# One stage for the gated recurrence of prompt and samples, the experts' rows added by TensorE, and one group of modulation weights moved to an earlier stage

## The chip, the cores and the metric

The kernel runs on one NeuronCore of one Trainium2 chip. The metric is the device time of one execution in microseconds; the kernel before has a median of 1935.73 us over three runs. Five engines work side by side: PE (TensorE, matmuls; its weight loads are PEld), DVE (VectorE), ACT (ScalarE), POOL (GpSimd) and SP (SyncE, which here only issues transfers). Each works through its own queue in program order, and semaphores order them among each other. PE's clock is granted at one of two levels, 1.2 or 2.4 GHz; the profile shows it as 0.5 or 1.

## The reference, cut to what matters

A step of a two-layer decoder, all in float32: a prompt of 512 tokens and 8 samples of one token each, width 1024. Layer 0 mixes by gated linear attention, layer 1 by differential attention over a cache; each layer ends with a mixture of 16 experts, of which every token takes two.

```python
def gla_recurrent(q, k, v, g, s0):          # the 8 samples, one step
    s = jnp.exp(gt)[..., None] * s + kt[..., None] * vt[..., None, :]
    return s, jnp.einsum('bhk,bhkv->bhv', qt, s)
...
sh1, sc1, g1, sh2, sc2, g2 = jnp.split(c @ w_ada[l] + b_ada[l], 6, axis=-1)
x = layer_norm(DEEPNORM_ALPHA * x + g1[:, None, :] * mix, ln_mix_g[l], ln_mix_b[l])
xm = modulate(x, sh2, sc2)
ff = moe_ffn(xm, w_router, b_router, w_exp_gate[l], w_exp_up[l], w_exp_down[l])
x = layer_norm(DEEPNORM_ALPHA * x + g2[:, None, :] * ff, ln_ffn_g[l], ln_ffn_b[l])
```

The state of the samples is 8 batches x 4 heads, each 128 x 256.

## The kernel before

The program is a row of stages, each a block whose engines all meet at its end: modulation, projection, recurrence of the prompt, recurrence of the samples, output (`stage_mix_output`), routing, experts, combine, decoder (layer 1's attention), and again output, routing, experts, combine. Tokens stand in five tiles (`TILES`): four of 128 and one of 8.

**Recurrence, prompt** (L593 on). Four chunks. DVE makes decays and factors, ACT their exponents (L720 to L726), PE transposes (L758), scores (L764 to L771), the new state's products (L780) and outputs (L788, L789); DVE adds the state (L688) and ACT copies outputs (L736). SP first fills unused slots of `y_rows` (L805), waits for that transfer, and then loads the samples' states (L590), 4 MB.

**Recurrence, samples** (`stage_gla_sample`). For every batch PE spreads the values over 128 partitions (L881, two banks of 512 columns), DVE decays the state (L859) and adds key times value (L863), four heads each; then PE multiplies the new state by the query (L890), and SP stores it (L832). The output weights load here (L905). At the end DVE copies the output rows (L869).

**Output.** PE projects a tile at a time (L1070); DVE gates, normalises and modulates (L1111 to L1130, L1011 to L1016); PE turns the modulated rows (L1060). SP writes the rows out, one transfer of 512 KB per tile, which the experts gather later (L941); these buffers alternate, so that tile n's row waits for the transfer of tile n - 2. `m.v` and `m.r`, in the upper part of `arena_w`, are read for the last time when the fifth tile has been turned.

**Routing.** PE makes the logits (L1261, L1266); DVE works 11 us on the choice of experts, then PE counts (L1272). Meanwhile SP loads five 2 MB pieces of the first experts' weights (L1170).

**Combine** (`stage_combine`). POOL gathers the two experts' rows of a tile (L1694), two tiles ahead of use. ACT multiplies the first by its weight (L1730), DVE adds the second times its weight (L1708), gates (L1111), adds the residual (L1119), takes the moments (L1123, L1125); ACT normalises (L1153), DVE multiplies by the gain (L1138, one tile late) and POOL adds the bias (L1144). In layer 0 the stage also makes two groups of modulation vectors (class `Ada`, `ada_groups=(8, 10)`): for each a bias and four 2 MB pieces of `w_ada` are loaded (L190, L192) and PE multiplies them (L203, L207). Group 10's four pieces are not loaded before group 8's products are done.

## Time and profile before

| | us |
|---|---|
| median of three runs (lowest, highest) | 1935.73 (1934.38, 1936.28) |
| the profiled execution's own time | 1931.71 |
| its span, first to last instruction | 1929.8 |
| recurrence, both stages | 284.6 to 370.0 |
| output and routing of layer 0 | 370.0 to 496.7 |
| experts of layer 0 | 496.7 to 812.7 |
| combine of layer 0 | 812.7 to 884.1 |
| decoder | 884.1 to about 1415 |
| output, routing and experts of layer 1 | about 1415 to 1871.1 |
| combine of layer 1 | 1871.1 to 1929.8 |

In a timeline row stand the start, the duration, the engine, the line, the operation, what it writes and reads, how many such instructions the row joins, and in brackets how long the engine sat idle before it and who ended that. A float32 matmul shows as two records, so that x32 are 16 matmuls.

### The profile page before, as it was taken

To read this page: it belongs to the slowest core of one execution; us is meant where nothing else is said; L and a number is where in the kernel's file an instruction comes from. 1 tells how busy PE (TensorE), PEld (TensorE's weight loads), DVE (VectorE), ACT (ScalarE), POOL (GpSimd) and SP (SyncE) were. 2 spreads that over 40 slices of the span, in tenths; PEclk is the share of its full clock that TensorE was granted. 3 is DMA by queue.
4 is the path that set the end of the run, shared out by engine and by line. 5 is a ranking of instruction groups with operands and counts; after the bars stand their busy time and mean duration, and the time that the engine had idled before them with its cause. 6 is when DMAs were issued, how large, how long until landed. Compare 5 with 4: busy or idle time off the path is not lost. (4 is left out here: it accounts for less than half of the span.)

```text
span 1929.8 us, 22099 instructions
## 1 busy us (share of the span) xinstructions
PE 1521.2 (79%) x7374; PEld 709.2 (37%) x7375; DVE 733.9 (38%) x1284; ACT 418.1 (22%) x908; POOL 349.3 (18%) x270
## 2 busy tenths in 40 slices
PE   5899986695689999646999887777596599989950
PEld 2333335142333333203466563444343233333320
DVE  1001127675300000075846577995275300000018
ACT  1001014221121222222120002334431021212222
POOL 0000000000100000033735566650000000000004
PEclk8999998597799999967999997888798699999985
DMA  8572604604599999699789999985503499999962
GB/s 314 225 275 111 263 36 152 233 23 185 224 425 422 392 382 427 275 370 344 276 306 402 408 383 412 351 316 182 186 17 129 188 417 384 418 420 400 430 242 89
DMA packets 123149, 551.66 MB, mean 286 GB/s; under 512 B 16469, under 2 KB 46022, under 8 KB 101419
## 3 DMA queue, kind: packets, MB, share of 16 engines
q1 hardware_dynamic: 94530, 492.46, 64.4%
q10 hardware_dynamic: 19584, 37.28, 5.1%
q0 software_dynamic: 8944, 20.76, 3.0%
q8 instruction: 51, 0.84, 0.2%
q14 instruction: 40, 0.33, 0.0%
HBM read 521.82 MB, written 40.03 MB: 291 GB/s over the span
## 5 line engine op out<-in xcount | busy, mean ns | idle before, releaser
L1576 PE MATMUL ps<-arena_w,arena_r 128*64 128x512 f32 x1600 | 361.7, 608 | 28.8 <-issue 23.9
L1576 PEld LDWEIGHTS ps<-arena_w,arena_r 128*64 128x64 f32 x1600 | 121.1, 140 | 262.6 <-issue 256.5
L1558 PE MATMUL ps<-arena_w,arena_r 128*64 128x512 f32 x800 | 181.5, 601 | 19.4 <-ACT arena_r L1606 19.4
L1653 DVE TENSOR_TENSOR arena_r<-arena_r,ps 128x512 f32<-128x512 f32 x38 | 26.1, 687 | 419.1 <-ACT arena_r L1623 419.1
L1959 POOL TENSOR_TENSOR arena_w<-arena_w,arena_r 128x1024 f32<-128x1024 f32 x48 | 115.5, 2409 | 104.0 <-DMA arena_w<-in_cache_k_dram 103.7
L1959 POOL TENSOR_TENSOR arena_r<-arena_r 128x1024 f32<-128x1024 f32 x48 | 115.9, 2418 | 54.7 <-DMA arena_r<-in_cache_k_dram 54.6
L2012 PE MATMUL ps<-arena_w,xt 128*128 128x256 f32 x512 | 123.4, 403 | 1.4 <-ACT xt L2185 1.4
L450 PE MATMUL ps<-arena_w,xt 128*128 128x512 f32 x256 | 113.8, 600 | 1.0 <-DVE arena_w L531 0.6
L1070 PE MATMUL ps<-arena_w,xt 128*128 128x512 f32 x256 | 111.4, 593 | 0.0
L2012 PEld LDWEIGHTS ps<-arena_w,xt 128*128 128x128 f32 x512 | 102.5, 203 | 17.9 <-ACT xt L2185 1.5
L1507 POOL COPY small<-idx 128x1 int32 (+1 forms) x38 | 7.0, 184 | 516.9 <-PE ps L1524 456.0
L1558 PEld LDWEIGHTS ps<-arena_w,arena_r 128*64 128x64 f32 x800 | 54.8, 138 | 119.9 <-issue 98.1
L1646 DVE COPY arena_r<-ps 128x512 f32<-128x512 f32 x38 | 26.3, 691 | 186.9 <-PE ps L1558 186.9
L1622 ACT ACTIVATE arena_r<-ps 64x512 f32<-64x512 f32 x38 | 22.4, 589 | 338.2 <-PE ps L1576 338.2
L2347 DVE TENSOR_REDUCE arena_r<-arena_w 128x16 f32<-128x1024 f32 x64 | 76.6, 1212 | 23.5 <-POOL arena_w L1959 23.4
L2347 DVE TENSOR_REDUCE arena_r<-arena_r 128x16 f32<-128x1024 f32 x64 | 76.6, 1210 | 17.3 <-POOL arena_r L1959 17.2
L2024 PE MATMUL ps<-arena_m,arena_r 128*16 128x512 f32 x512 | 67.8, 652 | 7.2 <-DMA arena_m<-in_cache_v_dram 7.2
L450 PEld LDWEIGHTS ps<-arena_w,xt 128*128 128x128 f32 x256 | 48.0, 191 | 66.3 <-issue 65.6
L1070 PEld LDWEIGHTS ps<-arena_w,xt 128*128 128x128 f32 x256 | 48.0, 190 | 59.1 <-issue 59.1
L415 PE MATMUL ps<-xt,arena_w 128*128 128x512 f32 x128 | 59.1, 616 | 4.0 <-PEq L249 3.7
L1234 POOL MEMSET arena_r<- 128x2048 f32 x2 | 3.6, 1806 | 308.1 <-POOLq L927 308.1
L2004 PE MATMUL ps<-xt,arena_w 128*128 128x512 f32 x128 | 56.9, 601 | 0.0
(384 smaller groups left out, 1969.5 us busy)
## 6 DMA issues: line engine op xcount, KB each, us to landing
arena_w<-in_w_exp_gate_dram SPq DMA_DIRECT2D x38, 2048.0 KB, 13.6
arena_w<-in_w_exp_up_dram SPq DMA_DIRECT2D x38, 2048.0 KB, 19.1
arena_w<-in_w_exp_down_dram SPq DMA_DIRECT2D x38, 2048.0 KB, 17.5
arena_m<-in_cache_v_dram SPq DMA_DIRECT2D x128, 512.0 KB, 7.0
arena_w<-in_cache_k_dram SPq DMA_DIRECT2D x64, 512.0 KB, 9.0
arena_r<-in_cache_k_dram SPq DMA_DIRECT2D x64, 512.0 KB, 8.4
arena_w<-in_w_ada_dram SPq DMA_DIRECT2D x12, 2048.0 KB, 17.6
arena_m<-in_w_ada_dram SPq DMA_DIRECT2D x12, 2048.0 KB, 9.2
```

Source lines behind the costliest of these rows:

```text
L415: last = nc.tensor.matmul(m.ps[n % 2][:, :], w, m.xt[:, k, 0:SEQ], start=(k == 0), stop=(k == KT - 1))
L450: last = nc.tensor.matmul(m.ps[4 + n % 4][:, :], m.xt[:, k, i * P:(i + 1) * P], m.wr[c % 2][:, k, :], start=(k == 0), stop=(k == KT - 1))
L1070: last = nc.tensor.matmul(m.ps[(4 if n % 2 else 6) + c][0:r, :], m.xt[:, k, i * P:i * P + r], w.of(k, c), start=(k == 0), stop=(k == KT - 1))
L1558: last = nc.tensor.matmul(psy[c][at:at + 64, :], ht[u][:, k, 64 * (1 - a):64 * (2 - a)], wd[u][:, k, c * 512:(c + 1) * 512], start=(k == 0 ...
L1576: last = nc.tensor.matmul(ps[at:at + 64, :], xgt[u][:, k, 64 * a:64 * (a + 1)], w[u][:, k, :], start=(k == 0), stop=(k == KT - 1), tile_po ...
L1646: V.tensor_copy(ys[u][:, 0:512], psy[0][:, :]).then_inc(y_v, 1)
L1653: V.tensor_tensor(hs[u], es[u], psu[:, :], ALU.mult).then_inc(h_ok, 1)
L1959: G.tensor_tensor(kp[n % RING], kp[n % RING], qb[b % 2], ALU.mult).then_inc(pp_ok, 1)
L2004: last = nc.tensor.matmul(bank[:, :], w[:, k, part * P:(part + 1) * P], m.xt[:, k, 0:SEQ], start=(k == 0), stop=(k == KT - 1))
L2012: last = nc.tensor.matmul(bank[:, i * CW:(i + 1) * CW], m.xt[:, k, t], w[:, k, :], start=(k == 0), stop=(k == KT - 1))
L2024: last = nc.tensor.matmul(PSO[n][32 * g:32 * g + C, :], PR[b % 2][:, GRP * q + g, :], vp[GRP * (v % 2) + g][:, n * 512:(n + 1) * 512], sta ...
L2347: V.tensor_reduce(out=S[b % 2][:, j, :], in_=kp[n % RING].rearrange("p (c d) -> p c d", d=DHB), axis=AX.X, op=ALU.add).then_inc(ks_ok, 1)
```

## The change

It has four parts, and one that goes with them. (1) Prompt and sample recurrence are one stage, `stage_gla`. The states load first and the fill of `y_rows` after them, from another source, awaited only at the end. A sample's output is computed from the old state with decayed queries, plus the product of query and key times the value; a sample's state takes one product of PE (K = 8 rows) and one operation of DVE that decays and adds. The products use seven banks of PSUM, and two alternating banks for transposed keys become one. Four copies on ACT and four selections on POOL prepare the masked keys. The output weights load in four parts. (2) The combine of both layers scales and adds the two rows on PE, by diagonal matrices that ACT makes from the weights; the normalisation is two operations of DVE. POOL only gathers, and gathers again once PE has read the rows. (3) Group 10 of `Ada` loads in layer 0's output stage, between the store of the first and the second tile, and is multiplied in the routing, after the logits and before the counts. (4) The first experts' up and down weights wait for these products, since they use the same buffers. In the routing POOL's clearing of a buffer moves to the end.

```diff
+            def sample(u):
+                b, h = u // HA, u % HA
+                if h == 0:
+                    v.wait_ge(st_in[b // 2], 16)
+                    wait(v, so_mm, 1 - b)
+                v.wait_ge(kv_mm, u + 1)
+                V.scalar_tensor_tensor(out=st[:, u, :], in0=st[:, u, :], scalar=eg[:, h, b:b + 1], in1=kv_ps[u % 7],
+                                       op0=ALU.mult, op1=ALU.add).then_inc(st_ok, 1)
...
             state(2)
+            for u in range(3):
+                sample(u)
             state(3)
+            for u in range(3, NS * HA):
+                sample(u)
+            sample_rows()
...
             key_rows(1)
+            s.wait_ge(kr_mm, 1)
+            for h in range(HA):
+                nc.scalar.copy(masked[h], so_ps[32 * h:32 * h + NS, 0:P].unsqueeze(1).to_broadcast([NS, NS, P])).then_inc(kr_ok, 1)
             exponents(2)
...
                 pe.wait_ge(fac_ok, i + 1)
-                wait(pe, kl_ok, i - 1)
+                wait(pe, kl_ok, i)
...
+            def sample(u):
+                b, h = u // HA, u % HA
+                wait(pe, st_ok, u - 6)
+                nc.tensor.matmul(kv_ps[u % 7], masked[h][:, b, :], m.v[32 * h:32 * h + NS, NTT - 1, h * DVA:(h + 1) * DVA],
+                                 start=True, stop=True, tile_position=(32 * h, 0)).then_inc(kv_mm, 1)
...
             outputs(1)
+            sample_outputs()
             factors(2)
             factors(3)
             outputs(2)
+            pe.wait_ge(ks_ok, HA)
+            pe.wait_ge(kl_ok, NTL)
+            pe.wait_ge(at_ok, NTL)
+            for u in range(3):
+                sample(u)
             outputs(3)
+            pe.wait_ge(s_ok, NTL)
+            pe.wait_ge(o_ev, NTL)
+            for u in range(3, NS * HA):
+                sample(u)
@@ stage_mix_output
                 sp.dma_start(m.xmD[i * P:i * P + r, :], xm[n % 2][0:r, :]).then_inc(rows_out[n % 2], 16)
+                if n == 0 and ada is not None:
+                    sp.wait_ge(tr, NTT)
+                    for step in range(Ada.STEPS):
+                        ada.load(sp, step)
@@ stage_route
-            load_expert(sp, m, weights, 0, 0)
-            load_expert(sp, m, weights[0:2], 1, 1)
+            load_expert(sp, m, weights[0:1], 0, 0)
+            load_expert(sp, m, weights[0:1], 1, 1)
+            if ada is not None:
+                sp.wait_ge(ada.used, Ada.STEPS)
+            load_expert(sp, m, weights[1:3], 0, 0)
+            load_expert(sp, m, weights[1:2], 1, 1)
...
             last.then_inc(mm, 1)
+            if ada is not None:
+                for step in range(Ada.STEPS):
+                    ada.product(pe, step)
             pe.wait_ge(sel_ok, 1)
@@ stage_combine
+            for i, r in TILES:
+                pe.wait_ge(dg_ok, i + 1)
+                pe.wait_ge(y_in[i % 2], 32 * (i // 2 + 1))
+                wait(pe, f_ok, i - 1)
+                for n in range(2):
+                    for c in range(2):
+                        last = nc.tensor.matmul(y_ps[i % 2][n][0:r, :], dg[c][i][0:r, 0:r], y[i % 2][c][0:r, n * 512:(n + 1) * 512],
+                                                start=(c == 0), stop=(c == 1))
+                last.then_inc(y_mm, 1)
+                if i:
+                    for step in range((i - 1) * steps // (NTT - 1), i * steps // (NTT - 1)):
+                        ada.product(pe, step)
...
                 if i >= 2:
-                    g.wait_ge(f_ok, i - 1)
+                    g.wait_ge(y_mm, i - 1)
...
-                v.wait_ge(y1_ok, i + 1)
-                y1, y2 = y[i % 2]
-                nc.vector.scalar_tensor_tensor(out=y1[0:r, :], in0=y2[0:r, :], scalar=m.wts[0:r, 1, i:i + 1],
-                                               in1=y1[0:r, :], op0=ALU.mult, op1=ALU.add)
-                v.drain()
-                ln.mixed(v, i, r, [y1[:, 0:512], y1[:, 512:1024]]).then_inc(f_ok, 1)
-                ln.stats(v, i, r)
-                if i:
-                    ln.shift(v, *TILES[i - 1])
-            ln.shift(v, *TILES[-1])
+                v.wait_ge(y_mm, i + 1)
+                ln.mixed(v, i, r, y_ps[i % 2]).then_inc(f_ok, 1)
+                ln.normalised(v, i, r)
@@ build
-        stage_combine(nc, ctx, m, 0, a, ada_groups=(8, 10), vectors=(6, 7, 12, 13), dec=dec)
+        stage_combine(nc, ctx, m, 0, a, ada_groups=(8,), vectors=(6, 7, 12, 13), dec=dec)
```

Three places where instructions stand otherwise. The first is DVE at the end of the recurrence. Before, from the last scores to the output rows (L688 adds the prompt's state, L859 and L863 the samples'; the pair of rows comes eight times):

```order
L679 TENSOR_TENSOR arena_r<-ps,arena_r 128x512 x2
L688 SCALAR_TENSOR_TENSOR arena_w<-arena_w,small,ps 128x256 x8
L626 UNCONDITIONAL_BRANCH
L850 UNCONDITIONAL_BRANCH
L852 MEMSET arena_r 128x256
L854 COPY arena_r<-arena_w 128x4x8
L859 TENSOR_SCALAR arena_m<-arena_m,arena_r 128x256 x4
L863 SCALAR_TENSOR_TENSOR arena_m<-ps,arena_w,arena_m 128x256 x4
```

and with the change (L736 adds the prompt's state, L675 is the one operation per sample and head, L685 the output rows):

```order
L727 TENSOR_TENSOR arena_r<-ps,arena_r 128x512 x2
L736 SCALAR_TENSOR_TENSOR arena_w<-arena_w,small,ps 128x256 x4
L675 SCALAR_TENSOR_TENSOR arena_m<-arena_m,arena_w,ps 128x256 x3
L736 SCALAR_TENSOR_TENSOR arena_w<-arena_w,small,ps 128x256 x4
L675 SCALAR_TENSOR_TENSOR arena_m<-arena_m,arena_w,ps 128x256 x29
L680 COPY arena_w<-ps 128x1
L685 SCALAR_TENSOR_TENSOR arena_w<-arena_w,ps 8x256 x4
```

The block's end between the two parts is gone, and 64 operations on the states are 32, three of them ahead of the prompt's last state. The second place is SP's queue in layer 0's output stage, before (-) and after (+):

```order
-L941 DMA xm_rows<-arena_r 8x1024
-L941 DMA xm_rows<-arena_r 128x1024 x4
+L962 DMA arena_r<-in_w_router_dram 128x8x16
+L962 DMA arena_r<-in_b_router_dram 128x16
+L965 DMA xm_rows<-arena_r 8x1024
+L190 DMA arena_r<-in_b_ada_dram 1x2048
+L192 DMA arena_w<-in_w_ada_dram 128x2x2048 x4
+L965 DMA xm_rows<-arena_r 128x1024 x4
```

The four 2 MB loads stand ahead of four of the five row stores. The third is PE in layer 0's combine, before

```order
L203 MATMUL ps<-arena_r,ones 32x512 x4
L207 MATMUL ps<-arena_w,small 32x512 x32
L203 MATMUL ps<-arena_r,ones 32x512 x4
L207 MATMUL ps<-arena_w,small 32x512 x32
L1684 MATMUL ps<-ident,arena_r 128x9 x32
```

and after (L1739 are the diagonal products, four a tile):

```order
L1739 MATMUL ps<-arena_r,xt 128x512 x8
L203 MATMUL ps<-arena_r,ones 32x512 x4
L207 MATMUL ps<-arena_w,small 32x512 x8
L1739 MATMUL ps<-arena_r,xt 128x512 x4
L207 MATMUL ps<-arena_w,small 32x512 x8
L1739 MATMUL ps<-arena_r,xt 128x512 x4
L207 MATMUL ps<-arena_w,small 32x512 x8
L1739 MATMUL ps<-arena_r,xt 8x512 x4
L207 MATMUL ps<-arena_w,small 32x512 x8
L1750 MATMUL ps<-ident,arena_r 128x9 x32
```

One group's products are gone, and the others stand between the tiles' sums, each behind the next tile's.

## Rows read from the trace of the kernel before

**Rows 1.** Layer 0's combine: us, busy PE, PEld, DVE, ACT, POOL; clock, DMA share, GB/s.

```profile
812.70:884.10 71.40, 29.79 (x176) 7.79 (x176) 42.52 (x59) 15.64 (x18) 26.70 (x15) 0.62 0.93 358
```

**Rows 2.** Timeline of DVE, 332 to 368 us: start us, us, line, op, tiles.

```profile
332.08 1.66 DVE L688 SCALAR_TENSOR_TENSOR arena_w<-arena_w,small,ps 128x256 f32<-128x256 f32 x4 [3.53 <-PE ps L780]
...
343.75 1.66 DVE L863 SCALAR_TENSOR_TENSOR arena_m<-ps,arena_w,arena_m 128x256 f32<-128x256 f32 x4 [2.12 <-PE ps L881]
...
366.37 1.72 DVE L869 COPY arena_w<-ps 8x256 f32<-8x256 f32 x4 [1.16 <-PE ps L890]
```

**Rows 3.** Waits of DVE, 285 to 385 us: total us, times, longest.

```profile
DVE arena_m L863 <- PE ps L881: 2.6, 3, 2.1
```

**Rows 4.** Timeline of SP's queue in the same stages.

```profile
296.30 5.95 SPq L590 DMA_DIRECT2D arena_m<-in_state_gla_dram  x4
...
370.04 0.30 SPq L336 DMA_DIRECT2D arena_m<-mod_rows  x1
```

**Rows 5.** Timeline of PE in the same stages.

```profile
316.17 0.66 PE L758 MATMUL ps<-ident,arena_w 128*128 128x128 f32 x4 [2.86 <-DVE xt L674]
...
345.46 1.04 PE L890 MATMUL ps<-arena_m,arena_r 128*8 128x256 f32 x8
...
346.43 2.08 PE L881 MATMUL ps<-arena_w,arena_r 8*128 8x512 f32 x4
```

**Rows 6.** Timeline of ACT in the same stages.

```profile
304.83 0.63 ACT L720 ACTIVATE arena_w<-arena_r 128x512 f32<-128x512 f32 x1 [2.08 <-DVE arena_r L659]
...
335.54 1.07 ACT L736 COPY arena_w<-ps 128x512 f32<-128x512 f32 x2 [4.11 <-PE ps L789]
```

**Rows 7.** Timeline of DVE in layer 0's output stage.

```profile
440.58 1.23 DVE L1011 TENSOR_TENSOR arena_r<-x_res,arena_m 128x1024 f32<-128x1024 f32 x1 [1.31 <-ACT x_res L1153]
...
448.89 1.29 DVE L1111 TENSOR_TENSOR arena_r<-ps,arena_m 128x512 f32<-128x512 f32 x2 [3.35 <-PE ps L1070]
```

**Rows 8.** Timeline of PE in layer 0's output stage and routing.

```profile
418.04 1.04 PE L1060 MATMUL ps<-ident,arena_r 8*128 8x8 f32 x8
...
434.95 13.90 PE L1070 MATMUL ps<-arena_w,xt 128*128 128x512 f32 x32
...
481.12 0.71 PE L1272 MATMUL ps<-arena_r,ones 128*128 128x80 f32 x2 [10.93 <-DVE arena_r L1365]
...
505.13 1.12 PE L1576 MATMUL ps<-arena_w,arena_r 128*64 128x512 f32 x2 [1.16 <-ACT arena_r L1600]
```

**Rows 9.** Timeline of PE in layer 0's combine, to the decoder's start.

```profile
824.69 1.93 PE L203 MATMUL ps<-arena_r,ones 1*32 1x512 f32 x8 [16.61 <-DMA arena_w<-in_w_ada_dram]
...
826.55 3.64 PE L207 MATMUL ps<-arena_w,small 128*32 128x512 f32 x16
...
831.84 1.92 PE L207 MATMUL ps<-arena_w,small 128*32 128x512 f32 x16 [1.65 <-DMA arena_w<-in_w_ada_dram]
...
884.18 1.02 PE L2104 MATMUL ps<-ident,x_res 8*128 8x8 f32 x8 [4.95 <-PEq L57]
```

**Rows 10.** Timeline of ACT in layer 0's combine.

```profile
824.08 1.15 ACT L1730 ACTIVATE arena_r<-arena_r,wts 128x1024 f32<-128x1024 f32 x1 [14.79 <-DMA arena_r<-y_rows,dest]
...
831.65 1.15 ACT L1730 ACTIVATE arena_r<-arena_r,wts 128x1024 f32<-128x1024 f32 x1 [6.42 <-DMA arena_r<-y_rows,dest]
```

**Rows 11.** Timeline of SP's queue in layer 0's combine.

```profile
848.78 0.25 SPq L190 DMA_DIRECT2D arena_r<-in_b_ada_dram  x1
```

**Rows 12.** Timeline of DVE in layer 1's combine.

```profile
1902.92 1.28 DVE L1708 SCALAR_TENSOR_TENSOR arena_r<-arena_r,wts 128x1024 f32<-128x1024 f32 x1
...
1904.28 3.27 DVE L1111 TENSOR_TENSOR arena_r<-arena_r,arena_m 128x512 f32<-128x512 f32 x2
...
1912.32 1.27 DVE L1708 SCALAR_TENSOR_TENSOR arena_r<-arena_r,wts 8x1024 f32<-8x1024 f32 x1
```

**Rows 13.** Timeline of ACT in layer 1's combine.

```profile
1878.62 1.15 ACT L1730 ACTIVATE arena_r<-arena_r,wts 128x1024 f32<-128x1024 f32 x1 [10.90 <-DMA arena_r<-y_rows,dest]
```

**Rows 14.** Timeline of SP's queue at the end.

```profile
1927.65 0.34 SPq L1757 DMA_DIRECT2D out_y_sample_dram<-x_res  x1
```

More of the change, by code:

```diff
@@ L698, in _ @@
             differences(1)
+            decayed_queries()
             products(0)
@@ L812, in _ @@
             sp.wait_ge(s_out, 16)
[L815 to L828 removed]
+            sp.wait_ge(o_mm, NTL)
@@ L1288, in _ @@
             nc.scalar.activation(E, L, ACT.Exp).then_inc(ex_ok, 1)
+            if ada is not None:
+                ada.evacuate(s, nc.scalar.copy, 0)
+                ada.store(s, 0)
+                ada.finish(s)
         @block.vector
@@ L1676, in _ @@
         def _(pe):
-            for step in range(len(ada_groups) * Ada.STEPS):
-                ada.product(pe, step)
+            steps = len(ada_groups) * Ada.STEPS
+            for i, r in TILES:
[10 more added lines that the diff above has]
+                        ada.product(pe, step)
             for n, row in enumerate(rows):
```

229 lines of the change are left out of this document (115 added, 114 removed).

## The prediction, written before the changed kernel ran

> **What bounds the kernel now.** I read the stretches by stage first, then each engine's timeline in the stages that the change touches, and last the waits. No engine bounds the whole: every stage ends at its own wait, and what is saved in one moves the next forward whole, since all engines meet at a block's end. The samples' recurrence fills the time from the prompt's last state, 333.74, to 370.04: DVE starts its first four L863 at 343.75 and the output copies L869 at 366.37, eight batches of four L859 and four L863, 2.8 us each [rows 2], with 2.6 us of waiting for PE in all [rows 3]; the next stage's first transfer is issued at 370.04 [rows 4]. Layer 0's combine takes 71.4 us with the transfer engines 93% busy [rows 1], with 16 MB of modulation weights in it. Layer 1's combine has no such weights: from 1878.62, when the first gathered rows are there [rows 13], to the last store's issue at 1927.65 [rows 14], it is a chain of DVE, 9.40 us from one tile's L1708 to the next's [rows 12]. In layer 0's output stage PE sets the pace (32 records of L1070 in 13.90 us, then DVE waits 3.35 us for PE) [rows 7, 8], and from there on the transfers are nearly idle until the routing.
>
> **Term 1, the recurrence: 12.9 us saved.** The new stage goes on from where the prompt's part goes now, but the prompt's part itself gets later. ACT makes four copies of 8 x 1024 out of PSUM. Two copies of 512 columns take 1.07 us [rows 6], so each costs about that, 4.3 us together; ACT idles 2.08 us before the exponents L720 that follow [rows 6], so these and the output copies behind them come 2.3 us later, and PE's second outputs wait for that copy. PE then makes the samples' outputs: 8 batches of L890's form, 1.04 us each at the lower clock [rows 5], 8.3 us; the clock here is the higher one for most of the time, and I take 4.4 us. PE idles 2.86 us before the next transposes at 316.17 [rows 5], which come 3.7 us later by this (2.3 + 4.4 - 2.86 = 3.8). DVE's fourth factors come 1.9 us later through ACT, and PE's last scores are held by both; I carry 2.1 us. The one bank for transposed keys costs nothing: the copy that it waits for is 0.58 us long and stands behind 3 us of factors on DVE. The last prompt state ends at 332.08 + 1.66 = 333.74, ACT's last copies at 336.6 [rows 2, 6]; both 2.1 us later, and three samples' products (1.3 us) go ahead: PE begins the other 29 at 340.0. DVE's operation reads one SBUF and one PSUM tile as L863 does, 1.66 / 4 = 0.41 us, with 0.40 from start to start. So 29 x 0.40 = 11.6 and 0.6 for the first hand-over give 352.2; the sum and four short operations (L869's four take 1.72) end at 354.6, and the last state's store, at 355. Now the block goes on 370.04 - 368.09 = 1.95 us after DVE's last copy [rows 2, 4]; so 357.1, 12.9 us earlier. Bounds: PE at the lower clock for the outputs, 4 us more delay, 9; no delay of the prompt's part, 15.5. The states load at once, not 11.7 us later [rows 4]; they were not waited for in either case. The output weights come in four parts, the last one at about 349, and are read some 10 us into the next stage: nothing.
>
> **Term 2, layer 0's output stage: 0.** SP waits until the fifth tile is turned, 419 [rows 8], and then issues four 2 MB loads; the store of the second tile stands behind them in the same queue, with 2.3 us of issuing and 8.4 MB of data ahead. At the 0.41 MB/us of the busy stretches that is 20 us, so the store lands at about 441. DVE rewrites that buffer at 440.58 and has 3.35 us to spare before the last tile [rows 7]. Bound: 29 us for the loads, since in layer 0's combine, beside gathers, the second piece comes 7.15 us after the first [rows 9]; the store lands at 451; 10.4 - 3.35 = 7 us lost.
>
> **Term 3, the routing: 0.** PE is done with the logits at 470.2 and waits 10.93 us for DVE [rows 8]. The group costs a bias of 1.93 us and four steps of 3.64 (lower clock) or 1.92 (higher) [rows 9]: 9.6 to 16.5 us. In the combine the clock rises after the first step, so I take 1.9 + 1.9 + 3 x 1.92 = 9.6: hidden, with 1.3 us to spare. Without it, 16.5 - 10.93 = 5.6 us come on the path, since the counts stand behind the products in PE's queue and DVE waits for them. The first up and down weights are issued at 480, 15 us later, and three pieces take 15.7 us: 496, before the experts' first product at 505.13 [rows 8]. ACT's copy and stores end there too.
>
> **Term 4, layer 0's combine: 7 us saved.** Group 10's loads are gone, that begin at 848.78 [rows 11], when group 8's products are done, and hold the transfers to the end. What sets the end then? The first rows still land at 824.08 and the second at 831.65 [rows 10], as the transfers are as loaded as before: 8.4 MB of group 8, then at once 4.2 MB for the decoder and 4.2 MB of gathers, all done at 854 at 0.42 MB/us. PE adds a tile in four matmuls, 8 records; of L1070's form 32 take 13.90 us [rows 8], so 3.5 us at 2.4 GHz and 7.0 at 1.2 GHz. PE has been idle and starts low: 6.1 us for the first, and DVE begins at 830.3, not 825.3. Then the gathers hold it: a gather is issued when PE has read the tile before the last, and lands some 10 us after its issue under load. So the third tile is there at 844 and summed at 848.5, the fourth (behind a step of the group, 1.9 to 3.6 us) at 855.5, the fifth landed at 857.8 and summed at 863. DVE takes 7 us for it, ACT copies and stores the group's rows, and the stage ends at 873. PE idles 4.95 us before the decoder's first matmul at 884.18 [rows 9], some 4 us of it after the stage's end; so 877, 7 us earlier. Bounds: 13 (all sums at the higher clock, gathers in time: 824.1 + 3.5 + 5 x 6.94 + 4 = 866.3, and 4 for the group's rows and the stage change: 871) and 2 (the lower clock throughout, PE alone 56 us).
>
> **Term 5, layer 1's combine: 8.3 us saved.** A tile of DVE: 9.40 [rows 12] less L1708 (1.36 with its drain), less 1.98 (L1111's two take 3.27 beside POOL [rows 12] and 1.29 out of PSUM [rows 7]), less 0.08 and the 0.29 us wait for ACT, plus one 1024-wide operation of 1.25: 6.94 us. The start: rows at 1878.6, PE cold 6.1 us, 1884.8; five tiles end at 1919.5, and the last store goes out there, not at 1927.65 [rows 14]: 8.2, and 8.3 with the shorter tail. Bounds: 5 (each sum at 7.0 us, gathers chained behind it) and 11 (first sum 3.5 us). ACT's ten diagonal copies lie before 1878.6, with 10.9 us of idling there [rows 13]; were they on the path they would cost about 3 us.
>
> L1111 takes 3.27 us only in tiles in which POOL's L1144 runs. The Trainium skill (SBUF — State Buffer, "SBUF: two separate sides") says that DVE and GpSimd share one port pair as an exclusive lock, and that a gather issued from GpSimd needs it for its descriptors. The trace agrees for L1144; by that page the gathers remain a contender, which would leave some of the 1.98 us in.
>
> Speaking against the change, the lower clock: PE's first group step takes 3.64 us and the next 1.92 [rows 9]. The Trainium skill (TensorE: Matmul & The Clock Gate, "What's actually happening") says that the throttled 1.2 GHz is the default and activity releases it. If that kept PE low in a stage where it works under half of the time, terms 4 and 5 would be 2 and 5: the first rival.
>
> **Sum.** 12.9 + 0 + 0 + 7 + 8.3 = 28.2. The profiled execution took 1931.71 us, so 1903.5; the median of the runs is 4.0 above it, and I forecast 1906 for a median.
>
> **The rivals.**
> (a) PE stays at 1.2 GHz in the combines and gathers chain behind it: 12.9 + 2 + 5 = 20, so 1916. For it: granted clock 0.62 in layer 0's combine [rows 1]; against it: 831.84's step at 1.92 after an idle gap [rows 9]. 0.20.
> (b) The row stores land late behind the loads, 7 us, perhaps with the routing's 5.6: 28.2 less 7 to 12.6, 1913 to 1919. The Trainium skill (DMA: Bandwidth & Descriptors, "Queues, rings and completion order") has descriptors of one ring consumed in order; no row shows a small store behind large loads. 0.12.
> (c) More comes: the terms' upper bounds, 15.5 + 12 + 10 = 37.5, so 1898. 0.16.
> (d) Slower: the samples' loop does not run ahead. Seven banks part PE from DVE; if each of the 29 still costs a matmul (0.6 to 1.1) and an operation (0.41) in turn, 1.6 us each are 46 us for 11.6: 34.8 lost against 28.2, so 6.6 us above the median, 1942. It decides from 28.2 / 29 + 0.40 = 1.37 us a sample on. Against it: DVE waited for L881 only 2.6 us in eight batches, with two banks of lead [rows 3], and a pair of L881's takes PE 1.04 us for two heads [rows 5]. 0.03.
>
> **Numbers.** The forecast (24 to 33 us, 1901 to 1911) has 0.48, with (a) 0.20, (c) 0.16, (b) 0.12, (d) 0.03, and 0.01 for a change that comes to nothing. The range of 1894 to 1918 leaves out half of (b)'s tail, (d) and the far end of (c). A measurement of this kernel tells 0.2%, 3.9 us, from nothing: faster 0.96, same 0.01, slower 0.03.
>
> **What the changed profile would show.** Right: the output stage's first transfer near 357; the sample operations 0.40 us apart without waits; PE's counts in the routing still at 481 less 13; tiles of 7 us in the combines, and L1111 never above 1.4; the decoder 20 us earlier, the last store's issue 28 us earlier. Wrong if: sums of 7 us on every tile; DVE waiting before the fourth tile of the output stage; PE still at L192's products when DVE has chosen; or the samples' operations further than 0.5 us apart.

## The result, and the profile after

The changed kernel took 1907.19 us (median of 3 runs, 1902.56 to 1916.82), the kernel before 1935.73: a ratio of 0.9866, with a 95% interval of 0.9818 to 0.9913, so 28.5 us less. The forecast was 1906, in a range of 1894 to 1918. The profiled execution of the changed kernel took 1907.19 us, with a span of 1905.3. One run further down (the one with the output weights last) took 2032.78 us at a granted clock of 0.79, where its kernel otherwise shows 0.89 to 0.90, and is left out of that kernel's median.

Both profiles cut at the same places, each stage from its first transfer or first instruction to that of the next (us; the last one to the last store's issue). Each column is one execution; the experiments show how far a stage with the same code moves between executions, 2 to 8 us in the longest ones:

| stage | before | after | difference | forecast |
|---|---|---|---|---|
| recurrence | 85.5 | 75.8 | -9.7 | -12.9 |
| layer 0's output stage | 93.1 | 94.8 | +1.7 | 0 |
| layer 0's routing and experts | 349.5 | 352.2 | +2.7 | 0 |
| layer 0's combine | 71.5 | 60.0 | -11.5 | -7 |
| decoder, layer 1's output stage | 599.7 | 598.3 | -1.4 | 0 |
| layer 1's routing and experts | 387.9 | 390.4 | +2.5 | 0 |
| layer 1's combine | 55.8 | 47.2 | -8.6 | -8.3 |

**Recurrence.** The timelines of DVE and of SP's queue after (start us, us, line, op, tiles, idle time before), to be held against [rows 2, 4]:

```profile
339.98 11.45 DVE L675 SCALAR_TENSOR_TENSOR arena_m<-arena_m,arena_w,ps 128x256 f32<-128x256 f32 x29 [3.72 <-PE ps L853]
351.35 0.15 DVE L680 COPY arena_w<-ps 128x1 f32<-128x1 f32 x1
351.58 1.94 DVE L685 SCALAR_TENSOR_TENSOR arena_w<-arena_w,ps 8x256 f32<-8x256 f32 x4
```

```profile
340.49 3.50 SPq L903 DMA_DIRECT2D out_s_sample_dram<-arena_m  x3
344.10 0.49 SPq L929 DMA_DIRECT2D arena_w<-in_w_o_a_dram  x1
345.19 6.64 SPq L903 DMA_DIRECT2D out_s_sample_dram<-arena_m  x5
360.22 0.30 SPq L336 DMA_DIRECT2D arena_m<-mod_rows  x1
```

DVE takes 11.45 us for 29 heads, 0.395 each, in one row without a gap: PE runs ahead as forecast. But DVE is done at 353.5, and the next stage begins only 6.7 us later, where it was 1.95 before. The waits of SP's queue say for what (total us, times, longest):

```profile
SPq L917 <- DMA out_s_sample_dram<-arena_m: 6.4, 1, 6.4
```

The queue's owner waits 6.4 us for the last state's store to land; that store stands behind 1 MB of output weights and four other stores of 0.5 MB in one queue. Before the change the same wait was

```profile
SPq L826 <- DMA out_s_sample_dram<-arena_m: 2.6, 1, 2.6
```

**Layer 0's output stage.** DVE after, against [rows 7]:

```profile
425.21 1.29 DVE L1139 TENSOR_TENSOR arena_r<-ps,arena_m 128x512 f32<-128x512 f32 x2 [5.73 <-PE ps L1098]
...
435.78 1.23 DVE L1039 TENSOR_TENSOR arena_r<-x_res,arena_m 128x1024 f32<-128x1024 f32 x1 [5.56 <-DMA xm_rows<-arena_r]
440.66 1.28 DVE L1139 TENSOR_TENSOR arena_r<-ps,arena_m 128x512 f32<-128x512 f32 x2
```

The row store behind the group's four loads is awaited 5.56 us, in place of 1.31 us for ACT. The 3.35 us for PE that stood before the last tile are used up, so that 4.25 - 3.35 = 0.9 us lie on the path. The rest of the stage's 1.7 us has nothing to do with the loads, which are issued at 409. It lies in PE's products of the modulation vectors at the stage's start, before the change and after it:

```profile
380.87 4.69 PE L154 MATMUL ps<-arena_w,xt 128*32 128x512 f32 x32
```

```profile
371.04 5.47 PE L154 MATMUL ps<-arena_w,xt 128*32 128x512 f32 x32
```

The same 32 records take 4.11 to 5.56 us in the profiles of the other kernels, with and without the loads.

**Routing.** PE after, against [rows 8]:

```profile
461.99 1.93 PE L203 MATMUL ps<-arena_r,ones 1*32 1x512 f32 x8
463.85 8.58 PE L207 MATMUL ps<-arena_w,small 128*32 128x512 f32 x64
472.77 0.50 PE L1321 MATMUL ps<-arena_r,ones 128*128 128x80 f32 x2 [0.34 <-DVE arena_r L1418]
```

The group's products lie under DVE's choice of experts: PE still waits 0.3 us for DVE behind them. The granted clock was 0.50 for the bias and the first of them (461.9 to 466.0) and 0.93 for the rest.

**Layer 0's combine.** PE after, against [rows 9], and one row of windows (columns as in [rows 1]):

```profile
818.76 5.24 PE L1739 MATMUL ps<-arena_r,xt 128*128 128x512 f32 x8 [16.16 <-DMA arena_r<-y_rows,dest]
826.42 3.67 PE L1739 MATMUL ps<-arena_r,xt 128*128 128x512 f32 x8 [2.42 <-DMA arena_r<-y_rows,dest]
...
836.94 6.38 PE L1739 MATMUL ps<-arena_r,xt 128*128 128x512 f32 x8 [4.00 <-issue]
...
852.79 3.78 PE L1739 MATMUL ps<-arena_r,xt 8*8 8x512 f32 x8 [2.13 <-issue]
...
867.24 1.01 PE L2156 MATMUL ps<-ident,x_res 8*128 8x8 f32 x8 [3.93 <-PEq L57]
```

```profile
807.20:867.20 60.00, 35.80 (x144) 13.24 (x144) 33.79 (x54) 6.04 (x17) 11.95 (x11) 0.76 0.77 285
```

The transfers are busy 77% of the stage instead of 93%: they no longer fill it to its end. They still hold it in one place. The third tile's gather is issued when PE has read the first tile, and DVE waits for its sum:

```profile
843.36 1.29 DVE L1139 TENSOR_TENSOR arena_r<-ps,arena_m 128x512 f32<-128x512 f32 x2 [5.25 <-PE ps L1739]
```

Three of the sums take 3.7 to 3.8 us, the other two 5.2 and 6.4.

**Layer 1's combine.** DVE's first and last tile, and the last store, against [rows 12, 14]:

```profile
1868.15 1.29 DVE L1139 TENSOR_TENSOR arena_r<-ps,arena_m 128x512 f32<-128x512 f32 x2 [12.79 <-PE ps L1739]
...
1875.16 1.28 DVE L1139 TENSOR_TENSOR arena_r<-ps,arena_m 128x512 f32<-128x512 f32 x2
...
1896.09 1.27 DVE L1139 TENSOR_TENSOR arena_r<-ps,arena_m 8x512 f32<-8x512 f32 x2
```

```profile
1903.10 0.34 SPq L1809 DMA_DIRECT2D out_y_sample_dram<-x_res  x1
```

One tile to the next takes 7.0 us instead of 9.4, and DVE waits for nothing after its first.

### The profile page after: what moved, and what is told of

Same layout as the page of the kernel before. It is cut to its first block and busy times, and to the rows that moved or that the text cites. A ratio compares the mean times of both kernels' runs of the same rounds, so it can differ in the third digit from the quotient of the medians.

```text
span 1905.3 us, 22323 instructions
## 1 busy us (share of the span) xinstructions
PE 1556.4 (82%) x7502; PEld 729.9 (38%) x7503; DVE 704.6 (37%) x1243; ACT 404.9 (21%) x914; POOL 320.0 (17%) x262
## 5 line engine op out<-in xcount | busy, mean ns | idle before, releaser
L1629 PE MATMUL ps<-arena_w,arena_r 128*64 128x512 f32 x1600 | 365.8, 614 | 28.6 <-issue 23.7
L1611 PE MATMUL ps<-arena_w,arena_r 128*64 128x512 f32 x800 | 183.4, 606 | 19.3 <-ACT arena_r L1659 19.3
L2011 POOL TENSOR_TENSOR arena_r<-arena_r 128x1024 f32<-128x1024 f32 x48 | 115.4, 2410 | 56.5 <-DMA arena_r<-in_cache_k_dram 56.2
L1739 PE MATMUL ps<-arena_r,xt 128*128 128x512 f32 (+1 forms) x80 | 42.7, 687 | 41.4 <-DMA arena_r<-y_rows,dest 30.5
```

The costliest lines, as they stand in the source:

```text
L1611: last = nc.tensor.matmul(psy[c][at:at + 64, :], ht[u][:, k, 64 * (1 - a):64 * (2 - a)], wd[u][:, k, c * 512:(c + 1) * 512], start=(k == 0 ...
L1629: last = nc.tensor.matmul(ps[at:at + 64, :], xgt[u][:, k, 64 * a:64 * (a + 1)], w[u][:, k, :], start=(k == 0), stop=(k == KT - 1), tile_po ...
L1739: last = nc.tensor.matmul(y_ps[i % 2][n][0:r, :], dg[c][i][0:r, 0:r], y[i % 2][c][0:r, n * 512:(n + 1) * 512], start=(c == 0), stop=(c == 1))
L2011: G.tensor_tensor(kp[n % RING], kp[n % RING], qb[b % 2], ALU.mult).then_inc(pp_ok, 1)
```

## The experiments

Two theories stood at the start. The first is the prediction's: each term is a chain in its own stage, and layer 0's combine was held by the transfers of group 10. The rival: PE's sums and DVE's shorter row of work are what shortened that combine, and the group's place matters little. A second pair was about the 3 us missing in the recurrence: bytes ahead of the last store, or stores that are slow whatever stands ahead.

The kernels of one list shared a chip, and the kernel before ran beside each list: the first four; then the loads in pairs, the eight products, one bank and four pairs; then the last two. On the second chip the changed kernel itself was not run, so there a median is compared through its ratio to the kernel before (0.985 to 0.9866 for the changed kernel).

**The changed kernel again** (no edit).

> The changed kernel as it is, timed again in more rounds, because its three runs lay 14 us apart (1902.56 to 1916.82) where those of the kernel before lay 2 us apart. If the terms of the sum hold, 24.6 us earlier in the profile, the median is again 1904 to 1910. If the spread is its own (the experts' stage of layer 0 took 2.7 us more in the profile of after than before, at a clock of 0.96 against 0.98), single runs again lie 5 us or more above the fastest, and the difference shows in the long TensorE stages and not in the stages that were edited; if it was chance of one chip, the runs lie within 4 us.

Measured: 1906.15 us (5 runs, 1903.3 to 1910.08), ratio 0.985 (0.9826 to 0.9875). The kernel before, run 23 times beside the first four kernels, spread from 1927.1 to 1942.5, so three runs within 2 us say little, and the scatter is no property of the change. Where it comes from, the stage cuts show: over the profiles, in all of which their code is untouched, the decoder with layer 1's output stage lasts 597.1 to 604.9 us, layer 1's routing and experts 387.8 to 390.4. The +2.7 of layer 0's routing and experts is of this kind too: those stages take 352.1 us in the next kernel, in which they are exactly those of before. The recurrence varies too: 75.4 to 75.8 us in three of the profiles with its code unchanged, 77.1 in one, and 78.8 to 79.0 in three, this one among them. PE's timeline in this one:

```profile
304.79 1.99 PE L838 MATMUL ps<-arena_w,arena_r 128*128 128x256 f32 x8
310.09 3.78 PE L847 MATMUL ps<-arena_w,arena_r 128*128 128x256 f32 x8 [3.31 <-DVE arena_r L727]
313.66 3.17 PE L838 MATMUL ps<-arena_w,arena_r 128*128 128x256 f32 x8
```

In the first profile L847 takes 1.89 us there and the L838 behind it 1.97. After a wait of 3.31 us PE works at half its pace, 3.78 us for 1.89, and the products behind are slow too.

That wait has a cause in the rows, and it lies on POOL and DVE. POOL's selections of the masked keys, which are new with the change, run beside DVE's row of subtractions (L701 to L707). In the first profile they begin when only the last of these is still to come:

```profile
303.81 0.42 DVE L706 TENSOR_TENSOR arena_r<-arena_r 128x256 f32<-128x256 f32 x1
304.15 1.58 DVE L707 TENSOR_TENSOR arena_r<-arena_r 128x512 f32<-128x512 f32 x1
303.83 5.28 POOL L655 TENSOR_SCALAR_AFFINE_SELECT arena_w<-arena_w 8x1024 f32<-8x1024 f32 x4 [17.96 <-ACT arena_w L799]
```

and in this one three are still to come, and each of them takes 0.9 us longer; the operation that PE waits for, L727, stands behind them:

```profile
305.39 1.32 DVE L705 TENSOR_TENSOR arena_r<-arena_r 128x256 f32<-128x256 f32 x1
306.63 1.30 DVE L706 TENSOR_TENSOR arena_r<-arena_r 128x256 f32<-128x256 f32 x1
307.86 1.57 DVE L707 TENSOR_TENSOR arena_r<-arena_r 128x512 f32<-128x512 f32 x1
305.29 5.11 POOL L655 TENSOR_SCALAR_AFFINE_SELECT arena_w<-arena_w 8x1024 f32<-8x1024 f32 x4 [17.51 <-ACT arena_w L799]
```

All ten profiles of kernels with this stage divide the same way. In five, PE's second transposes (L816) take 1.11 or 1.12 us, POOL begins 1.03 us behind DVE's L701, and one operation of DVE is stretched. In the other five the transposes take 0.66 us, so that ACT and POOL come half a microsecond sooner, and three operations are stretched; these are the profiles with the stage at 77 us or more (75.8 in the one that has the output weights last). So it goes by the pace at which PE makes these transposes, and here the quicker transposes give the longer stage. That is read from the profiles; no run moved POOL's selections to prove it, and what decides PE's pace there stays open.

**The new combine alone**, on the kernel before: the combine and the normalisation's methods of the change, group 10 still in layer 0's combine.

```
 # the kernel before, with
 stage_combine, LayerNorm     # as changed
 stage_combine(..., 0, a, ada_groups=(8, 10), ...)   # as before
```

> The kernel before with the new combine alone; group 10 of the modulation weights is still loaded in layer 0's combine, and the recurrence is the old one. Theory 1 (as in the prediction, the transfers hold layer 0's combine while group 10 is in it): layer 1's combine gives 8.5 us, layer 0's at most 2, so 10 us less than before, 1925. Theory 2 (PE's sums and the shorter row of work on DVE are what shortened layer 0's combine, the group's place matters little): layer 0's combine about 61 us here too, 20 us less, 1916.

Measured: 1930.14 us (12 runs), beside 1934.02 for the kernel before; ratio 0.9976 (0.9959 to 0.9992). By stage, layer 0's combine takes 71.75 us (71.5 before), layer 1's 48.6 (55.8 before): theory 1. DVE in layer 0's combine:

```profile
856.53 1.29 DVE L1111 TENSOR_TENSOR arena_r<-ps,arena_m 128x512 f32<-128x512 f32 x2 [0.51 <-PE ps L1698]
870.82 1.28 DVE L1111 TENSOR_TENSOR arena_r<-ps,arena_m 8x512 f32<-8x512 f32 x2 [7.22 <-PE ps L1698]
882.10 0.22 DVE L1736 TENSOR_SCALAR small<-ps 128x64 f32<-128x64 f32 x1 [4.30 <-PE ps L1709]
```

PE's sum for the fifth tile stands in its queue behind two steps of group 10, which wait for their weights; DVE, faster per tile, now waits 7.22 us for it and 4.30 more at the end, for the products of the group's last weights. The transfers are busy 92% of the stage. All of the new combine's gain in layer 0 is lost in the waits for them.

**Group 10 back in layer 0's combine**, on the changed kernel.

```
-stage_mix_output(..., router, ada=ada)
-stage_route(..., router, ada=ada)
-stage_combine(..., ada_groups=(8,), ...)
+stage_mix_output(..., router)
+stage_route(..., router)
+stage_combine(..., ada_groups=(8, 10), ...)
```

> The changed kernel with group 10 back in layer 0's combine: no modulation load in the output stage, no products in the routing. Theory 1: layer 0's combine lasts 69 to 71 us again instead of 60, the output stage gets its 1.7 us back, so 8 us slower than the changed kernel, 1915. Theory 2: the combine stays near 61 us, and with the 1.7 us given back the time is 1905 to 1907, the same as the changed kernel. Under both the wait of DVE for the row store in the output stage (5.56 us) is gone.

Measured: 1922.71 us (12 runs), ratio to before 0.9943 (0.9925 to 0.9961). This is 16.6 us above the changed kernel on the same chip, twice what theory 1 gave. Its combine lasts 74.4 us instead of 60.0, and its output stage 92.9 instead of 94.8 (DVE waits 3.33 us for PE again, none for the row store): 12.5 us by stage. That figure is itself good to some 3 us, since the same combine lasted 71.75 us in the run before. The other 4 lie within the scatter of the later stages.

Along the steps before, new combine, new recurrence, moved group, the medians fall by 3.9, 7.4 and 16.6 us; by stage the same steps are about 7 (layer 1's combine), 10 and 12.5. The last step shifts 8 MB of loads into a stretch with idle transfers and saves nothing by itself in instructions, and it comes last: what it gives the old combine was not run. An estimate from the kernel before: its combine ends with an addition on POOL,

```profile
876.30 2.33 POOL L1144 TENSOR_TENSOR x_res<-x_res,arena_m 8x1024 f32<-8x1024 f32 x1 [1.15 <-DVE x_res L1138]
```

at 878.6, and with 2.1 us to the decoder, as after the change, it could not have ended before 880.7. So the move alone would be worth at most 3.5 us there and the new combine alone is worth nothing; the 11.5 us come only with both.

**Output weights behind the last store**, on the changed kernel.

```
-            w_out.load(sp, 0)
             for b in range(3, NS):
                 sample_store(b)
+            w_out.load(sp, 0)
```

> The changed kernel with one edit in the recurrence: the first part of the output weights (1 MB) is issued after the last state's store, not ahead of the last five. In the changed kernel the queue's owner waits 6.4 us for the last store to land (2.6 us before the change). Theory A (this tail is the 1 MB and the four stores ahead of the last one, by bytes in flight): 1 MB at 0.41 MB/us is 2.5 us, the wait falls to about 4 us, the next stage begins 2.5 us earlier, 1904.7, unless the weights, now 2.5 us later, are awaited there. Theory B (the stores' own landing is slow, whatever stands ahead of them): the wait stays at 6 us or more and the time is unchanged.

Measured: 1904.61 us (5 runs, 1901.49 to 1916.2), ratio 0.986 (0.9828 to 0.9892). In the profile the wait falls, as in theory A, and by more than its 2.5 us:

```profile
SPq L917 <- DMA out_s_sample_dram<-arena_m: 2.5, 1, 2.5
```

The recurrence lasts 72.6 us instead of 75.8, and the output stage 94.9, so its weights are not missed. From the last store's issue to the next stage it is 5.1 us instead of 8.4, where it was 4.4 before the change. The saving of 3.2 us is there in the stage and not to be told from nothing in the median (1.5 us less).

**Group's loads in two pairs**, on the changed kernel.

```
 if n == 0 and ada is not None:
     sp.wait_ge(tr, NTT)
-    for step in range(Ada.STEPS):
-        ada.load(sp, step)
+if n < 2 and ada is not None:
+    for step in range(2 * n, 2 * n + 2):
+        ada.load(sp, step)
```

> The changed kernel with the four 2 MB loads of group 10 in two pairs in the output stage: two behind the first tile's row store, two behind the second's. Theory A (rival b of the prediction: in one queue, the row store lands only behind the 8 MB ahead of it, and DVE's rewrite of the buffer waits, 5.56 us in the profile of the changed kernel of which 3.35 were idle before): DVE's wait for the row store goes, PE is again what DVE waits for, 3 us or so before the last tile, and the output stage is 93 us instead of 94.8, so 1 to 2 us less than the changed kernel. Theory B (what makes the stage longer is the load on the transfer engines as such, or the clock): no change, or the wait moves to the next tile's row store.

Measured: 1910.22 us (5 runs), ratio 0.9873 (0.9852 to 0.9893). In the stage, theory A: 92.6 us, and DVE waits as before the change:

```profile
429.41 1.23 DVE L1040 TENSOR_TENSOR arena_r<-x_res,arena_m 128x1024 f32<-128x1024 f32 x1 [1.31 <-ACT x_res L1194]
437.71 1.29 DVE L1140 TENSOR_TENSOR arena_r<-ps,arena_m 128x512 f32<-128x512 f32 x2 [3.34 <-PE ps L1099]
```

Of the 2.2 us by which the stage is shorter, 0.9 are the loads'. They are DVE's wait of 5.56 us less the idle time that was there anyway. The other 1.3 us are again PE's L154 at the stage's start, 4.14 us here and 5.47 in the first profile, ahead of the loads. The median did not follow: the five runs lie 8.8 us apart (1904.11 to 1912.89), and 1 us can't be read from them.

**Eight products before the first sum**, on the changed kernel (they go to an unused bank).

```
+            for n in range(8):
+                nc.tensor.matmul(m.ps[3][:, :], m.ident[:, :], m.lnr[:, 0, 0:512], start=True, stop=True)
             for i, r in TILES:
```

> The changed kernel with eight more 128x512 products of PE into an unused bank at the start of each combine, while PE waits 12 to 16 us for the first gathered rows (they add nothing to the result). Theory A (the first sums are slow because PE comes to them at the lower clock: the first takes 5.24 us, the second 3.67): the first sum takes 3.7 us in both combines, layer 1's combine is 1.5 to 2 us shorter, layer 0's not much, since the gathers hold its third tile; 1904. Theory B (the first sum is slow because the second gather of the tile lands late, not because of the clock): it stays at 5.2 us and the time at 1906. If the eight products end too early, the clock falls again before the rows land, and A shows less.

Measured: 1906.49 us (4 runs), ratio 0.9854 (0.9831 to 0.9877). PE in layer 0's combine:

```profile
806.26 8.79 PE L1734 MATMUL ps<-arena_m,ident 128*128 128x512 f32 x16 [4.65 <-PEq L1543]
817.68 3.67 PE L1741 MATMUL ps<-arena_r,xt 128*128 128x512 f32 x8 [2.63 <-DMA arena_r<-y_rows,dest]
825.34 5.37 PE L1741 MATMUL ps<-arena_r,xt 128*128 128x512 f32 x8 [3.98 <-DMA arena_r<-y_rows,dest]
...
834.39 3.67 PE L1741 MATMUL ps<-arena_r,xt 128*128 128x512 f32 x8 [0.84 <-issue]
```

The first sum takes 3.67 us instead of 5.24: theory A. PE slows again at the second, after 3.98 us of waiting, for which DVE waits 2.26 us; but since the third tile's gather is issued when the first sum is done, that one comes sooner and the third sum is no longer slow. This chain is worth more than forecast: the stage lasts 55.8 us, 4.2 less. Layer 1's is 46.6, 0.6 less, where 1.5 to 2 were expected. PE's rows there say why:

```profile
1854.07 8.80 PE L1734 MATMUL ps<-arena_m,ident 128*128 128x512 f32 x16 [4.67 <-PEq L1543]
1862.70 7.03 PE L1741 MATMUL ps<-arena_r,xt 128*128 128x512 f32 x16
```

The eight products take 8.8 us (the next eight of the same form, the first two sums, take 7.0), and the first sum begins behind them without a wait, 8.0 us after the first gather's issue, where it began 6.6 us after it without them. So 1.4 us of the gain are spent on the products themselves. In the median nothing is seen; this profile had the longest decoder stage of all, 604.9 us, and its DVE keeps to within 1.8 us of the changed kernel's, ahead or behind, for the first 375 us of it, is 2.0 behind at 416 and 5.7 at 467. So the loss is not at the seam with the combine; what causes it stays open.

**One bank for the samples' products**, on the changed kernel: the price of the slower rival.

```
-    kv_ps = [m.ps[n][:, 0:DVA] for n in (0, 2, 3, 4, 5, 6, 7)]
+    kv_ps = [m.ps[n][:, 0:DVA] for n in (0,)]
...
-                wait(pe, st_ok, u - 6)
+                wait(pe, st_ok, u + 1 - len(kv_ps))
```

> The changed kernel with one bank of PSUM for the samples' products instead of seven, so that PE cannot run ahead of DVE: the price of the prediction's slower rival. By the prediction's price a sample then costs 1.6 us, so 29 take 46 us instead of 11.45, and the time is 1941. By the durations in the profile of the changed kernel (0.37 us of PE, 0.40 us of DVE) and some 0.1 us for each hand-over it would be 1.0 us a sample, 29 us, 1924. Above 1.37 us a sample the change would have been a loss.

Measured: 1948.95 us, ratio 1.0071 (1.0043 to 1.0098), 2 runs, slower than before the change. All but the first two of the 29 on DVE read like this one:

```profile
347.27 0.48 DVE L675 SCALAR_TENSOR_TENSOR arena_m<-arena_m,arena_w,ps 128x256 f32<-128x256 f32 x1 [1.31 <-PE ps L853]
```

1.79 us a head, 0.48 at work and 1.31 waiting: more than the prediction's price of 1.6, and well above the 1.37 from which the change loses. PE works at the lower clock here (0.51 from 343 to 392) and takes 1.21 or 1.22 us for each product. The three samples ahead of the last state met it at the higher clock, and there a head takes 1.27:

```profile
334.37 0.69 PE L853 MATMUL ps<-arena_w 8*128 8x256 f32 x2 [0.57 <-DVE arena_m L675]
335.11 0.48 DVE L675 SCALAR_TENSOR_TENSOR arena_m<-arena_m,arena_w,ps 128x256 f32<-128x256 f32 x1 [0.79 <-PE ps L853]
```

So about 0.5 of the 1.79 is the clock. As an estimate, 29 heads at 1.27 instead of 0.395 would lose 25.4 us against the 28.2 forecast, and the change would come out near nothing with one bank rather than as a loss. Either way the lead of seven banks is what the recurrence's gain stands on.

**Four pairs of buffers for the gathers**, on the changed kernel.

```
+    y += [[m.mod[:, u, c, :] for c in range(2)] for u in range(2)]
...
-                if i >= 2:
-                    g.wait_ge(y_mm, i - 1)
+                if i >= 4:
+                    g.wait_ge(y_mm, i - 3)
```

> The changed kernel with four pairs of buffers for the gathered rows in the combine instead of two (the other two lie in modulation rows that are no longer needed), so that four tiles' gathers are issued at the start. Theory A (what still holds layer 0's combine is the third tile's gather, issued only when PE has read the first and landed 10.5 us later: DVE waits 5.25 us for it): that wait goes, DVE works through five tiles at 7.0 us, the decoder starts 5 us earlier, 1901. Theory B (the rows land late because the transfers are full of group 8 and the decoder's weights, 12.6 MB, whenever they are issued): the first tiles land later, since eight gathers share the queue, and the wait only moves; 1905 to 1908. In layer 1's combine nothing changes under A (DVE has no waits there), under B the first rows may land later there too.

Measured: 1907.69 us (4 runs), ratio 0.9858 (0.9836 to 0.9879). Both theories hold in part. The third tile's rows are there in time, but the fourth's are late behind them:

```profile
833.57 3.67 PE L1740 MATMUL ps<-arena_m,xt 128*128 128x512 f32 x8 [1.24 <-issue]
837.17 1.92 PE L207 MATMUL ps<-arena_w,small 128*32 128x512 f32 x16
842.15 5.37 PE L1740 MATMUL ps<-arena_m,xt 128*128 128x512 f32 x8 [3.05 <-issue]
```

DVE's wait goes from 5.25 us at the third tile to 2.80 at the fourth, and the stage lasts 57.75 us, 2.3 less, not 5.

**The four edits together, and the changed kernel beside it.**

> The changed kernel with four edits of the runs so far together: the first part of the output weights behind the last state's store (stage 3.4 us shorter in the profile), the group's loads in two pairs (1.8 us), eight products of PE at the start of each combine (4.2 us in layer 0's, 0.6 in layer 1's), four pairs of buffers for the gathers (2.3 us in layer 0's combine alone, perhaps less beside the eight products, since the third tile is then waited for 0.3 us only). Theory A (each stage's saving moves what follows forward whole): 3.4 + 1.8 + 4.2 to 6 + 0.6 = 10 to 12 us less than the changed kernel on the same chip, 1895; by stage in its profile 93 us for the output stage, 54 to 56 for layer 0's combine, 46.6 for layer 1's. Theory B (the stages behind take it back: with each of these edits alone the median did not move, and the decoder's stage was 598 to 605 us long): those parts show in the stages but the median falls by less than 5 us, and the decoder's stage is again longer than 600.

> The changed kernel once more, on the same chip as the one with four edits, for that comparison. 1904 to 1909 as before; in its profile 94 to 95 us for layer 0's output stage, 60 for layer 0's combine, 47.3 for layer 1's, and 597 to 605 for the decoder's stage, whose code is that of the kernel before.

Measured on one chip, beside 1936.6 for the kernel before: 1896.72 us with the four edits (6 runs, ratio to before 0.9801, 0.9777 to 0.9825), 1909.1 without them (4 runs, 0.9864, 0.9843 to 0.9886). The intervals do not touch: 12.4 us less than the changed kernel, and 39.9 less than the kernel before. By the median that is theory A; the single edits, each 1 to 4 us in its stage, were too small for four to six runs. By stage in its profile: recurrence 75.8 us (79.0 in the neighbour's, both with the slow products), output stage 92.7 (93.6), layer 0's combine 56.5 (60.8), layer 1's 47.2 (46.9), decoder 598.75 (599.7). The buffers add nothing to the eight products in layer 0's combine, which is no shorter than the 55.8 with those alone, and layer 1's gains nothing in this pair. The edited stages account for 8 of the 12 us. The two profiled executions themselves lie only 4.8 us apart: this one, 1902.2 us, is one of the kernel's longer runs, the other is its kernel's shortest, and the stages with the same code are 3 us longer in it. Where the other 4 us of the medians come from the profiles don't show.

## Why the prediction was right, and where its terms were off

**Term 1, 12.9 forecast, 9.7 in the profile (6.5 in the repeat with the slow products).** The delay of the prompt's part (PE begins the other 29 samples at 339.3, for 340.0 forecast), the 0.40 us a head and the end of DVE's work (353.5 for 354.6) came nearly as worked out; PE's outputs for the samples took 3.63 us for the 4.4 assumed. The step that failed is "Now the block goes on 370.04 - 368.09 = 1.95 us after DVE's last copy". Before the change the stores came 2.8 us apart, and the wait for the last one was 2.6 us, partly beside DVE's last copies. (The prediction also put the 1.95 behind the last store's issue, 355, and not behind the last copy, 354.6, as it says; that is 0.5 of the sum.) Now the stores follow each other by four heads of 0.395 us, 1.6 us for 0.5 MB, and 1 MB of weights stands among them. With the weights behind, the wait is 2.5 us and the stage 3.2 shorter, as in the run: that 3.2 is the missing part. That the repeat saves only 6.5 us has another cause, for which the prediction has no term: the four selections on POOL stretch DVE's operations, in some executions on the path.

**Term 2, 0 forecast, 1.7 lost, of which 0.9 by the loads.** The mechanism was described and its size missed by a little: the store was to land at 441 for a rewrite at 440.58, and 3.35 us were to spare. It landed 4.25 us later than the rewrite could have begun, 444.8 in time of before, 0.9 more than the spare time. The other 0.8 are PE's L154 at the stage's start. The Trainium skill (DMA: Bandwidth & Descriptors, "Queues, rings and completion order") has descriptors of one ring consumed in order; both here (5.56 us, gone when two loads fewer stand ahead) and in term 1 (6.4 us, 2.5 when the weights go behind) the trace agrees. The second rival was thus real with 0.9 us for its 7.

**Term 3, 0.** PE's products ended 0.3 us before the counts, for 1.3 forecast: they take 8.58 us where 7.7 were carried, the first ones at the lower clock. The prediction's own reading, that the clock rises after the first step, would have given 1.9 + 3.64 + 3 x 1.92 = 11.3 us for bias and steps, more than the 10.93 it had; it wrote 1.9 for the first step. Bias and steps took 10.4 us, in the 10.7 between the end of the logits and the counts, so they were hidden by little. The experts' first product comes 41.5 us after the routing's start (42.0 before), so the later weights are not missed.

**Term 4, 7 forecast, 11.5.** In time of before, the timeline is as forecast: first sum 5.24 us (6.1), third ready at 848.8 (848.5), fourth at 854.3 (855.5), DVE at the fifth at 862.8 (863). The end was mis-sized: the decoder's first product was set at 877, but the group's rows are stored while DVE works on the last tile (ACT's stores at 862.34), and the decoder follows DVE's last operation by 2.1 us. 872.7 is the figure, 4.3 earlier. That it was the transfers which held this stage, the new combine alone shows, with a gain of nothing there; what the move of the group would give alone is an estimate (at most 3.5 us).

**Term 5, 8.3 forecast, 8.6.** Tiles 6.98 us apart for 6.94, first tile 5.6 us after the rows for 6.1. The gathers on POOL, named by the Trainium skill (SBUF — State Buffer, "SBUF: two separate sides") as a contender for DVE's port, cost DVE nothing that shows: L1139 takes 1.27 to 1.29 us in every tile, and L1147, which reads two tiles of SBUF and stands beside a gather at 825.43, 1.21 to 1.23. It is POOL's issue that stretches there, 1.95 us for 0.94. The selections in the recurrence did slow DVE, by 0.9 us each.

**The rivals.** (a) needed sums at the lower clock throughout; of the ten sums in the two combines seven take 3.6 to 3.8 us (two pairs are one row each, 9.03 and 7.19 us; I read the first as a slow and a fast one), and the slow ones stand behind waits. (c) had the size of term 4 nearly right (12 for 11.5), but not those of terms 1 and 5. Its sum, 15.5 + 12 + 10, takes 12 and 10 where the bounds of terms 4 and 5 were 13 and 11; with those it is 39.5, and 1896. (d)'s price is shown by the single bank (1.79 us for its 1.6); its condition did not occur. The forecast itself lies 1.5 us below its own sum: 1935.73 - 28.2 = 1907.5, for which 1906 was written. The sum of the terms, 28.2, met a profile shorter by 24.5 and medians that differ by 27.5 to 28.5: the misses of terms 1 and 2 (4.9 lost) and 4 and 5 (4.8 gained) cancel, and the 3.7 us between the sum and the profile are the differences of the stages to which it gave nothing, which the repeats show to be scatter. The forecast was as close as it was partly by that luck.

## What to carry to other kernels

Where a block ends when its last store has landed, count what stands ahead of that store in its queue, and issue loads for later behind it; the same holds for a load group put ahead of a small store that frees a buffer. A stage with the transfers at 93% may give nothing back for faster engines until bytes leave it: here the new combine was worth 0 with 8 MB more in the stage, and new combine and move together 11.5 us. The order in which parts are added decides what each seems worth. A new operation on POOL beside DVE is worth a look in the rows even when POOL has time to spare. When edits are worth 1 to 4 us and runs scatter by 10, read each in its stage and time them together.

## What the runs showed of the hardware that was not expected

- PE falls to the lower clock around short idle stretches, and the length of the wait alone does not tell when. Sums of the same form took 3.67 us behind waits of 2.42 and 2.63 us, and mostly 5.07 to 6.60 behind waits of 3.05 to 16.18 us. But behind 3.60 us two sums took 7.19 together (granted clock 1.00), and the fifth tile's sum in layer 0's combine, in the same place behind 2.10 to 2.16 us, took 3.78 in one profile, 4.89 in a second (0.72) and 6.98 in a third. Eight products ahead moved the slow one from the first tile to the second, and the mean granted clock of layer 0's combine rose from 0.76 to 0.84 with them.
- POOL's selections (8x1024 each, reading and writing SBUF) stretch DVE's operations with two inputs in SBUF by 0.9 us each: 0.42 to 1.32 and 1.30, 0.68 to 1.57. Gathers issued from POOL did not do that.
- A hand-over from PE to DVE and back costs 1.79 us a turn with one bank at the lower clock, for 0.48 us of work on DVE and 1.21 on PE, and 1.27 at the higher, with 0.69 on PE (L853 in pairs of records). With seven banks the same work runs at 0.395 a head.
- A program on one core has scatter of its own: 1927 to 1942 us for the kernel before on one chip, and in the profiles stages of 350 to 600 us whose length moved by 3 to 8 us with the same code.
